# The second layer's input projection in another column order, with the indexer between its pieces and two conditioning items loaded elsewhere

## The chip, the cores and the metric

The kernel runs on one core of one Trainium2 chip. The metric is the device time of one execution in microseconds (us). Five engines take part: TensorE (PE in the rows; its weight loads PEld), VectorE (DVE), ScalarE (ACT), GpSimd (POOL, hardly used here) and SyncE (SP), which issues nearly all of the transfers. Each engine runs its own instructions strictly in the order in which they were written and waits for others at semaphores.

## The reference

A model trunk of two layers for 256 tokens of width 1024, in fp32, with batch 1. Every sub-layer is RMSNorm, shift and scale from a conditioning vector `c`, the mixer or feed-forward part, a gate from `c`, and the residual. Layer 0 has dilated attention and an S5 state-space part, then a dense SwiGLU (width 2816). Layer 1, whose first half the change touches, is this:

```
proj = u @ w_in                                   # 1024 x 1880
q_r, q_n, ckv, k_r, q_i, k_i, w_i = split(proj)   # 256, 768, 256, 16, 512, 64, 8 columns
q_r = rope(q_r, 16 heads)   ckv = rms_norm(ckv, g_kv)   k_r = rope(k_r)
q_i = rope(q_i, 8 heads)    k_i = rope(k_i)             w_i = w_i * 8 ** -0.5
logits = einsum('bqhd,bsd->bqhs', q_i, k_i) * 64 ** -0.5
score  = einsum('bqh,bqhs->bqs', w_i, relu(logits)), causal
idx    = top_k(score, 64)                         # keys that a query may see
k_n, v = ckv @ w_uk, ckv @ w_uv                   # (the reference does this in latent form)
attention of 16 heads over the chosen keys; then @ w_out
```

After it comes a top-2-of-8 mixture of experts (width 3584 each) and a final norm.

## The kernel before

Weights pass through `ring`, five slots of 16 KB per partition (`NS0`), and two more (`ring_more`) in the experts. `item()` gives each weight piece the next slot in turn; SP issues the loads in one list, and each load first waits until the piece that last lay in its slot has been used. Wide products are made in three passes: a weight chunk is split into a high part (`high`, ACT, L1548: `w_hi`) and the rest (`low`, DVE, L1882: `w_lo`), and PE multiplies x_hi by w_hi, x_hi by w_lo and x_lo by w_hi (`mm3`, L783 to L785). There are four chunk buffers (`NB`), so ACT can convert chunk c of a piece only when PE is done with chunk c of the piece before. Each piece is one `item`: 8 rows of 128 inputs in four chunks of two; for two token tiles that makes 48 matmuls of the piece's width.

The order of the work is written out by hand for each engine. In time:

- Dense feed-forward of layer 0: a loop over 512-wide blocks (`ff_block`); it uses ring slots 4, 0 and 2. Slots 1 and 3 hold the conditioning items 12 and 13 (`ada_item`: 1024 x 512 pieces of `w_ada`), which PE multiplies with `c` (`matvec`, L808) before the loop. Item 13's `matvec` stands between the first gate product and the first up product; ACT copies its result out (`part_out`, L1490) before it converts the first up piece.
- Behind the loop: `matvec` of items 14 and 15, the last down product, the residual (DVE L1966, L1968), the norm (`norm_stats`, `norm_scale`, `norm_split`) and the shift and scale made from items 12 to 15.
- Layer 1's projection in six pieces in the order of the columns (`o_cols`): 256 (q_r), 384 and 384 (q_n), 272 (ckv, k_r), 512 (q_i), 72 (k_i, w_i). DVE applies rope to q between them (L1923 to L1928), ACT copies the rest out of PSUM.
- Then DVE finishes ckv and k_i, PE transposes ckv (L789), DVE copies it out with g_kv (L2189), PE makes k_n (L1204) and v (L1213), ACT and DVE copy them out. Then the indexer: ten transposes, eight heads of logits (L1236), relu on ACT (L1736), weighted sum on DVE (L2210, L2212), eight rounds of top-k on DVE (`max`, L2219, `match_replace`, L2223), and the mask (L2225 to L2227). Beside the top-k, PE transposes q and k and ACT copies them (L1740), and PE makes the first two heads' scores (`scores_pair`, L858).
- Attention in eight pairs of heads. DVE adds the mask and takes the maximum (`mask_max`, L1940), ACT takes the exponentials (`exps`, L1561), and so on; one conditioning item is multiplied in each pair. Then the output projection (L1289), the router, and eight experts of 21 weight pieces.

An fp32 matmul that is not of the three-pass kind is recorded twice in the trace: eight matmuls show as x16.

## Time and profile before

| What | us |
|---|---|
| median of 3 runs (range) | 1662.81 (1662.75 to 1663.93) |
| the profiled execution | 1659.71 |
| span of its core | 1657.9 |
| PE busy in the span | 1551.6 (94%) |
| DVE busy | 1259.0 (76%) |
| ACT busy | 1043.8 (63%) |
| mean granted TensorE clock | 0.975 of full |

The span is the time from the first to the last record of the core; 1.8 us of the execution lie around it. The chain of work that ended last lies on PE for 78% of the span, on DVE for 6% and on ACT for 5%. The experts alone fill 635 to 1658 us. The stretch that the change touches lies between 222 and 574 us: the start of the dense loop, its end at 418, the norm to 431, the projection to 480, keys, values and indexer to 523, attention to 574.

### The profile page before, as it was taken

Reading aid. Unit: us, or ns where it says so; the run is one execution under the profiler, and the core shown is the slowest. Engines: PE = TensorE matmul, PEld = TensorE weight load, DVE = VectorE, ACT = ScalarE, POOL = GpSimd, SP = SyncE. Lnnn points to the kernel's source line nnn. Section 1 sums busy time; section 2 is a strip of 40 time slices with the busy share of each in tenths; the row PEclk is TensorE's granted clock in tenths of the full one; section 3 lists DMA queues with packets and bytes.
Section 4 is the critical chain, followed back from the end, with each engine's and each line's share of the span. In section 5 each row is a group of like instructions: output and inputs, shape, how many; then the busy total and the mean of one; then the engine's idle time right before and its main releaser. Section 6 shows DMA issues by size and latency. Waiting matters only on the chain.

```text
span 1657.9 us, 22266 instructions
## 1 busy us (share of the span) xinstructions
PE 1551.6 (94%) x7619; PEld 1202.9 (73%) x7620; DVE 1259.0 (76%) x1719; ACT 1043.8 (63%) x1374; POOL 62.8 (4%) x90
## 2 busy tenths in 40 slices
PE   4899989999897888999999999999999999999997
PEld 2545468887764456888888888888888888888885
DVE  6896345443646237989989989989989989989987
ACT  3105444443425626778778778778778778778775
POOL 5251000000000000000000000000000000000000
PEclk9999999999888988999999999999999999999999
DMA  9635855545654837999999999999999999999970
GB/s 319 232 102 195 313 203 200 177 156 177 228 181 150 307 116 265 365 332 358 365 328 364 362 331 366 350 334 362 354 335 363 351 338 362 351 337 364 353 260 27
DMA packets 203752, 469.68 MB, mean 283 GB/s; under 512 B 5108, under 2 KB 11558, under 8 KB 203574
## 3 DMA queue, kind: packets, MB, share of 16 engines
q1 hardware_dynamic: 202656, 466.80, 77.9%
q0 software_dynamic: 400, 1.09, 0.3%
q10 hardware_dynamic: 646, 1.16, 0.2%
q8 instruction: 28, 0.46, 0.1%
q14 instruction: 22, 0.18, 0.0%
HBM read 467.98 MB, written 1.05 MB: 283 GB/s over the span
## 4 chain that ended last, share of the span: by engine, by line
PE 78%; DVE 6%; ACT 5%; issue 2%; DMA 0%; DVEq 0%; ACTq 0%
PE ps L783 22%; PE ps L785 21%; PE ps L784 21%; PE ps L789 2%; PE ps L1330 2%; DVE w_lo L1882 2%; PE ps L1289 2%; PE ps L1056 1%; ACT work L1778 1%; PE ps L808 1%; ACT w_hi L1548 1%; ACT uT L1561 1%; PE ps L828 1%; PE ps L1204 0%; PE ps L1399 0%
## 5 line engine op out<-in xcount | busy, mean ns | idle before, releaser
L1882 DVE TENSOR_TENSOR w_lo<-ring,w_hi 128x1024 fp32r<-128x1024 f32 (+2 forms) x576 | 667.4, 1192 | 116.3 <-ACT w_hi L1548 102.5
L1548 ACT ACTIVATE w_hi<-ring 128x1024 fp32r<-128x1024 f32 (+2 forms) x576 | 594.9, 1038 | 210.3 <-PE ps L785 206.7
L783 PE MATMUL ps<-w_hi,e_hi 128*128 128x512 f32 x896 | 356.6, 398 | 9.7 <-DVE w_lo L1882 9.7
L785 PE MATMUL ps<-w_hi,e_lo 128*128 128x512 f32 x896 | 350.5, 391 | 0.0
L784 PE MATMUL ps<-w_lo,e_hi 128*128 128x512 f32 x896 | 349.6, 390 | 0.0
L1882 DVE TENSOR_TENSOR w_lo<-ring_more,w_hi 128x1024 fp32r<-128x1024 f32 x192 | 228.8, 1220 | 40.5 <-ACT w_hi L1548 38.1
L1548 ACT ACTIVATE w_hi<-ring_more 128x1024 fp32r<-128x1024 f32 x192 | 201.6, 1067 | 70.6 <-PE ps L785 70.6
L783 PEld LDWEIGHTS ps<-w_hi,e_hi 128*128 128x128 f32 x896 | 168.8, 188 | 46.3 <-DVE w_lo L1882 13.2
L785 PEld LDWEIGHTS ps<-w_hi,e_lo 128*128 128x128 f32 x896 | 168.6, 188 | 36.7
L784 PEld LDWEIGHTS ps<-w_lo,e_hi 128*128 128x128 f32 x896 | 169.0, 189 | 33.6
L783 PE MATMUL ps<-w_hi,eT_hi 128*128 128x512 f32 x448 | 176.6, 394 | 5.7 <-DVE w_lo L1882 5.7
L784 PE MATMUL ps<-w_lo,eT_hi 128*128 128x512 f32 x448 | 174.6, 390 | 0.0
L785 PE MATMUL ps<-w_hi,eT_lo 128*128 128x512 f32 x448 | 174.6, 390 | 0.0
L783 PE MATMUL ps<-w_hi,x_hi 128*128 128x512 f32 (+4 forms) x288 | 104.2, 362 | 11.0 <-DVE x_lo L1917 6.5
L783 PEld LDWEIGHTS ps<-w_hi,eT_hi 128*128 128x128 f32 x448 | 84.1, 188 | 28.5 <-DVE w_lo L1882 11.8
L784 PE MATMUL ps<-w_lo,x_hi 128*128 128x512 f32 (+4 forms) x288 | 103.5, 359 | 0.0
L785 PE MATMUL ps<-w_hi,x_lo 128*128 128x512 f32 (+4 forms) x288 | 103.3, 359 | 0.0
L785 PEld LDWEIGHTS ps<-w_hi,eT_lo 128*128 128x128 f32 x448 | 84.1, 188 | 17.9
L784 PEld LDWEIGHTS ps<-w_lo,eT_hi 128*128 128x128 f32 x448 | 84.2, 188 | 16.5
L783 PEld LDWEIGHTS ps<-w_hi,x_hi 128*128 128x128 f32 x288 | 55.5, 193 | 19.4 <-issue 10.5
L808 PE MATMUL ps<-ring,c_col 128*32 128x512 f32 x384 | 50.3, 644 | 14.6 <-DMA ring<-in_w_ada 12.9
L785 PEld LDWEIGHTS ps<-w_hi,x_lo 128*128 128x128 f32 x288 | 55.7, 193 | 7.1
...
## 6 DMA issues: line engine op xcount, KB each, us to landing
...
```

The costliest lines, as they stand in the source:

```text
L783: mm(o, xh, wh, start=start, stop=False)
L784: mm(o, xh, wl, start=False, stop=False)
L785: return mm(o, xl, wh, start=False, stop=stop)
L789: return nc.tensor.transpose(o, i, ident[0:n, 0:n])
L808: w = mm(ps[bank][j:j + 32, :], c_col[:, k:k + 1].broadcast_to([P, 32]), ap[:, k, :], start=k < 4, stop=False, tile_position=(0, j))
L828: mm(ps[bank][:, :], sel_col.broadcast_to([P, P]), part, start=True, stop=True).then_inc(mod_summed, 1)
L1056: w = mm(ps[2 * n + t][:, :], catT[:, k, t * P:(t + 1) * P], ap[:, k, :], start=k == 4, stop=k == 3)
L1289: w = mm(ps[4 + 2 * n + t][:, :], ctxT[:, k, t * P:(t + 1) * P], ap[:, k, :], start=k == 0, stop=k == KD - 1)
L1330: w = mm(o, hn[:, t, d], sel[:, t, :], start=t == 0, stop=t == NT - 1)
L1548: fn(w, src, ACT.Copy).then_inc(hi_ready, 1)
L1561: w = fn(x, x, ACT.Exp, scale=SC, bias=stat[:, 12 + 2 * q + t:13 + 2 * q + t], **({"accum_out": stat[:, 18 + 2 * q + t:19 + 2 * q + t]} if ...
L1882: V.tensor_tensor(w_lo[0:n, c, 0:f], src, w_hi[0:n, c, 0:f].bitcast(F32), ALU.subtract).then_inc(lo_ready, 1)
```

## The change

The projection's 1880 columns are loaded in five pieces instead of six, in this order: q_i (512), then ckv, k_r, k_i and w_i together (344), then q in three pieces (352, 336, 336). PE transposes k_i and q_i after the third piece. The logits are made in four pairs of heads between the chunks of the last two pieces; ACT's relu and DVE's weighted sum stand between their conversions of those pieces. The top-k stands on DVE behind the weighted sum with nothing else of keys and values ahead of it. The copies of v, of the transposed ckv and of the keys' rope part go from DVE to ACT. On DVE and ACT the first piece (q_i) is split ahead of the residual and its norm. qiT, kiT and ckvT lie in another region, since the logits now run while x_hi and x_lo are in use. Conditioning items 14 and 15 take slots 1 and 3 and are loaded at the start of the dense loop; their `matvec` stays where it was. Item 13's `matvec` and its copy come after the first up product. Slot numbers of everything behind shift with it.

```diff
--- before
+++ after
...
+        qiT = WX.take(4, S)
+        kiT = WX.take(S)
+        ckvT = WX.take(2, S)
 
         W2 = Region(work, WORK, NT * D + 2 * KD * S)
...
         static_before = list(stream)
+        stream.clear()
+        n_then = n_item[0]
+        for (sec, half), back in zip(HALVES[2:4], (3, 1)):
+            n_item[0] = n_then - back
+            ada_item(1, sec, half)
+        n_item[0] = n_then
+        static_mid = list(stream)
...
-        for sec, half in HALVES[2:4]:
-            ada_item(1, sec, half)
-        o_cols = [(0, 256), (256, 384), (640, 384), (1024, 272), (1296, 512), (1808, 72)]
-        o_in = [item(A["o_w_in"][0, :, a:a + n], KD, n, "split") for a, n in o_cols]
+        NQI, NCK, NQ0, NQ1 = IH * HD, LAT + ROPE + HD + IH, 256 + 2 * NOPE, 7 * NOPE
...
+        def o_item(n, *cols):
+            s = n_item[0] % NS0
+            n_item[0] += 1
+            pieces, at_ = [], 0
+            for a, m in cols:
+                pieces.append((block_ap(s, KD, n)[:, :, at_:at_ + m], o_w_in[:, :, a:a + m]))
+                at_ += m
+            return (n, push(s, pieces, "split"))
+        o_qi = o_item(NQI, (1296, NQI))
+        o_ck = o_item(NCK, (1024, LAT + ROPE), (1808, HD + IH))
+        o_q = [o_item(NQ0, (0, NQ0)), o_item(NQ1, (NQ0, NQ1)), o_item(NQ1, (NQ0 + NQ1, NQ1))]
...
+            for e in static_mid:
+                load(e)
...
                 rows(q, (0, 1), n, (2, 3))
+                if first:
+                    pe.wait_ge(part_ready, 14)
                 ff_down(q + NCI, u0, first)
...
             rows_of(ff_first["gate"][2], 1, FW, 1, 1)
-            matvec(13, 6)
             pe.wait_ge(part_ready, 13)
             rows(ff_first["up"][2], (2, 3), FW, range(NCI))
-            pe.wait_ge(part_ready, 14)
+            matvec(13, 6)
             ff_block(0, True)
             with pe.Fori(1, FB - 2) as i:
                 ff_block(i, False)
...
-            for j, banks in enumerate(((0, 1), (2, 3), (4, 5), (6, 7), (0, 1), (2, 3))):
-                if j == 4:
-                    pe.wait_ge(rope_done, 6)
-                if j == 5:
-                    pe.wait_ge(nope_done, 6)
-                if j == 0:
-                    for t in range(NT):
-                        rows_of(o_in[0][1][2], banks[t], o_cols[0][1], t, 2)
+            o_rows = lambda it, banks, chunks=range(NCI): rows(it[1][2], banks, it[0], chunks)
+            for t in range(NT):
+                rows_of(o_qi[1][2], t, NQI, t, 2)
+            pe.wait_ge(mod_ready, 3)
+            o_rows(o_ck, (2, 3))
+            o_rows(o_q[0], (4, 5))
+            pe.wait_ge(ki_ready, 2)
+            pe.wait_ge(ckr_copied, 2)
+            for t in range(NT):
+                w = tr(ps[2][:, t * P:(t + 1) * P], k_iw[:, t, 0:2 * HD])
+            w.then_inc(idxT_done, 1)
+            pe.wait_ge(qi_ready, 2)
+            for pr in range(4):
+                for t in range(NT):
+                    w = tr(ps[pr // 2][:, (pr % 2) * S + t * P:(pr % 2) * S + (t + 1) * P],
+                           q_i[:, t, 2 * pr:2 * pr + 2, :].rearrange("p h d -> p (h d)"))
+                if pr % 2:
+                    w.then_inc(idxT_done, 1)
+            def logits(pr):
+                if pr == 0:
+                    pe.wait_ge(idxT_ready, 3)
                 else:
-                    if j == 1:
-                        pe.wait_ge(mod_ready, 3)
-                    rows(o_in[j][1][2], banks, o_cols[j][1], range(NCI))
-            pe.wait_ge(nope_done, 8)
+                    pe.wait_ge(relu_ready, 2 * pr)
+                for t in range(NT):
+                    for i in range(2):
+                        r = slice(HD * i, HD * i + HD)
+                        w = mm(ps[2 + i][:, KOFF[t]:KOFF[t] + KEYS[t]], qiT[r, pr, t * P:(t + 1) * P], kiT[r, 0:KEYS[t]],
+                               start=True, stop=True)
+                        if t == NT - 1:
+                            w.then_inc(logit_done, 1)
+            o_rows(o_q[1], (6, 7), (0, 1))
+            logits(0)
+            o_rows(o_q[1], (6, 7), (2,))
+            logits(1)
+            o_rows(o_q[1], (6, 7), (3,))
+            logits(2)
+            o_rows(o_q[2], (0, 1), (0,))
+            logits(3)
+            o_rows(o_q[2], (0, 1), (1, 2, 3))
+            pe.wait_ge(q_copied, 2)
+            pe.wait_ge(q_roped, 2)
             for t in range(NT):
                 pe.wait_ge(ckv_ready, t + 1)
...
+            pe.wait_ge(q_copied, 6)
+            pe.wait_ge(relu_ready, IH)
             for i in range(4):
                 t, half = i // 2, i % 2
                 for k in range(2):
...
             pending[0] = True
 
             pe.wait_ge(kn_ready, 4)
-            for pr in range(4):
-                for t in range(NT):
-                    w = tr(ps[4 + pr // 2][:, (pr % 2) * S + t * P:(pr % 2) * S + (t + 1) * P],
...
-            pe.wait_ge(idxT_ready, 3)
-            pe.wait_ge(v_ready, 4)
...
-                if i >= 2:
-                    pe.wait_ge(relu_ready, i - 1)
-                for t in range(NT):
...
-            pe.wait_ge(rope_done, 12)
+            pe.wait_ge(kr_set, 2)
             for i, src in enumerate((q_tok, kcat)):
                 for pr in range(8):
                     if i and pr % 2 == 0:
...
                     for t in range(NT):
                         w = tr(ps[4 + pr // 2][:, (pr % 2) * S + t * P:(pr % 2) * S + (t + 1) * P],
                                src[:, t, 2 * pr:2 * pr + 2, :].rearrange("p h d -> p (h d)"))
+                        release(w)
                     if pr % 2:
                         w.then_inc(qkT_done, 1)
+            pe.wait_ge(v_ready, 4)
             pe.wait_ge(qkT_ready, 12)
-            pe.wait_ge(relu_ready, IH)
             scores_pair(A_HEADS, qT1, kT1, 0, True)
 
...
                 if t:
                     part_out(12, parts1[:, 0, :], 2)
                 norm_hi(1, t)
-            part_out(13, parts1[:, 1, :], 6)
             item_high(ff_first["up"][2], *ff_first["up"][:2], ff_chunk_of(FW))
             act.wait_ge(chunk_done, NCI)
             silus(0)
+            part_out(13, parts1[:, 1, :], 6)
...
+            o_high(o_qi)
             norm_stats(2)
-            proj_end = lambda j: o_in[j][1][2] + NCI
...
+            for t in range(NT):
+                norm_hi(2, t)
+            o_high(o_ck)
+            o_rows_done(o_qi)
+            for t in range(NT):
+                fn(q_i[:, t, :, ROPE:], heads(ps[t][:, :], 8)[:, :, ROPE:], ACT.Copy).then_inc(qi_copied, 1)
+            o_high(o_q[0])
+            o_rows_done(o_ck)
+            for t in range(NT):
+                fn(ckr[:, t, :], ps[2 + t][:, 0:LAT + ROPE], ACT.Copy).then_inc(ckr_copied, 1)
...
+            o_high(o_q[1], (0, 1))
+            q_out(0, (4, 5), 256, 0, 2)
+            o_high(o_q[1], (2,))
+            for i in range(2):
+                act.wait_ge(idxT_done, i + 2)
+                fn(qiT[:, 2 * i:2 * i + 2, :], ps[i][:, :].rearrange("p (c s) -> p c s", c=2), ACT.Copy).then_inc(idxT_ready, 1)
+            o_high(o_q[1], (3,))
+            o_high(o_q[2], (0,))
+            relu(0)
+            relu(1)
+            o_high(o_q[2], (1, 2))
+            relu(2)
+            relu(3)
+            o_high(o_q[2], (3,))
+            relu(4)
+            relu(5)
+            q_out(1, (6, 7), 0, 2, 7)
+            relu(6)
+            relu(7)
+            for k in range(2):
+                act.wait_ge(ckvT_done, 1)
+                fn(ckvT[:, k, :], ps[4][:, k * S:(k + 1) * S], ACT.Copy, scale=g_kv[:, k:k + 1]).then_inc(ckvT_ready, 1)
+            q_out(2, (0, 1), 0, 9, 7)
+            for t in range(NT):
+                act.wait_ge(kr_ready, t + 1)
+                fn(kcat[:, t, :, 0:ROPE], kr_t[:, t, :].unsqueeze(1).broadcast_to([P, C_HEADS, ROPE]), ACT.Copy).then_inc(kr_set, 1)
...
+            for i in range(4):
+                t, half = i // 2, i % 2
+                act.wait_ge(kv_done, 5 + i)
+                fn(v1[:, t, half * 512:(half + 1) * 512], ps[i][:, :], ACT.Copy).then_inc(v_ready, 1)
             for i in range(8):
                 act.wait_ge(qkT_done, 5 + i)
                 dst = (qT1, kT1)[i // 4]
                 fn(dst[:, 2 * (i % 4):2 * (i % 4) + 2, :], ps[4 + i % 4][:, :].rearrange("p (c s) -> p c s", c=2),
                    ACT.Copy).then_inc(qkT_ready, 1)
+            fn(stat[:, 30:31], eps[:, 0:1], ACT.Exp)
             exps(A_HEADS, True)
...
-            for t in range(NT):
-                residual(t, 4, 1, (4 + 2 * t, 5 + 2 * t))
-            for t in range(NT):
-                dve.wait_ge(h_ready, 4 + 2 * t + 2)
-                norm_scale(2, t, 5 + t)
-            columns(0, 1, 10, 2)
...
+            o_low(o_qi)
+            for t in range(NT):
+                residual(t, 4, 1, (4 + 2 * t, 5 + 2 * t))
+            for t in range(NT):
+                dve.wait_ge(h_ready, 4 + 2 * t + 2)
+                norm_scale(2, t, 5 + t)
+            columns(0, 1, 10, 2)
+            dve.wait_ge(mod_ready, 3)
+            for t in range(NT):
+                norm_split(2, t)
+            o_low(o_ck)
+            q_index(0)
+            o_low(o_q[0], (0,))
+            q_index(1)
+            o_low(o_q[0], (1, 2, 3))
+            dve.wait_ge(ckr_copied, 2)
+            for t in range(NT):
+                k_index(t)
+            o_low(o_q[1], (0, 1))
+            for t in range(NT):
+                k_rope(t)
+                ckv_norm(t)
+            o_low(o_q[1], (2,))
+            dve.wait_ge(idxT_done, 1)
+            V.tensor_copy(kiT[:, :], ps[2][:, 0:S]).then_inc(idxT_ready, 1)
+            o_low(o_q[1], (3,))
+            q_rope(0)
+            o_low(o_q[2], (0,))
+            q_rope(1)
+            add_score(0)
+            add_score(1)
+            o_low(o_q[2], (1, 2))
+            add_score(2)
+            add_score(3)
+            o_low(o_q[2], (3,))
+            for i in range(4, IH):
+                add_score(i)
```

SP's list of loads, around the start and the end of the dense loop, before:

```order
L620 DMA ring<-in_ff_w_gate 128x8x512 [waits lo_ready]
L620 DMA ring<-in_ff_w_down 128x4x1024 [waits weights_used]
L620 DMA ring<-in_ff_w_up 128x8x512 [waits lo_ready]
...
L599 DMA ring<-in_ff_w_down 128x2x1024 [waits lo_ready]
L599 DMA ring<-in_w_ada 128x8x512 [waits lo_ready] x2
L599 DMA ring<-in_o_w_in 128x8x256 [waits ada_done]
```

and after:

```order
L644 DMA ring<-in_ff_w_gate 128x8x512 [waits lo_ready]
L644 DMA ring<-in_ff_w_down 128x4x1024 [waits weights_used]
L644 DMA ring<-in_ff_w_up 128x8x512 [waits lo_ready]
L623 DMA ring<-in_w_ada 128x8x512 [waits ada_done] x2
...
L623 DMA ring<-in_ff_w_down 128x2x1024 [waits lo_ready]
L623 DMA ring<-in_o_w_in 128x8x512 [waits lo_ready]
```

The two `w_ada` loads (items 14 and 15) stood at the end behind the last down piece and waited for the slots of gate and up; now they stand ahead of the loop, and the projection's first piece follows the down piece.

DVE between the last down product and the transposed norm, before:

```order
L1882 TENSOR_TENSOR w_lo<-ring,w_hi 128x512 [waits hi_ready] x4
L1966 TENSOR_TENSOR ps<-ps,gate_row 128x512 [waits gate_ready,chunk_done]
L1968 TENSOR_TENSOR h<-h,ps 128x512 [waits dve_steps]
...
L1874 COPY mod_b<-ps 128x8 [waits mod_summed]
L1875 SCALAR_TENSOR_TENSOR mod_a<-ps,g_col 128x8
L1882 TENSOR_TENSOR w_lo<-ring,w_hi 128x512 [waits hi_ready,mod_ready]
L1882 TENSOR_TENSOR w_lo<-ring,w_hi 128x512 [waits hi_ready] x3
L1908 TENSOR_SCALAR uT<-ps,mod_a,mod_b 128x128 [waits hnT_done]
```

and after:

```order
L1949 TENSOR_TENSOR w_lo<-ring,w_hi 128x512 [waits hi_ready] x4
L1949 TENSOR_TENSOR w_lo<-ring,w_hi 128x1024 [waits hi_ready,chunk_done]
L1949 TENSOR_TENSOR w_lo<-ring,w_hi 128x1024 [waits hi_ready] x3
L2033 TENSOR_TENSOR ps<-ps,gate_row 128x512 [waits gate_ready]
L2035 TENSOR_TENSOR h<-h,ps 128x512 [waits dve_steps]
...
L1941 COPY mod_b<-ps 128x8 [waits mod_summed]
L1942 SCALAR_TENSOR_TENSOR mod_a<-ps,g_col 128x8
L1975 TENSOR_SCALAR uT<-ps,mod_a,mod_b 128x128 [waits hnT_done,mod_ready]
```

The split of the projection's first piece has moved from behind the scale (`mod_a`) to ahead of the residual (`h`), and is 1024 instead of 512 elements wide per chunk.

PE between the projection and the attention's first scores, before (L1204 makes k_n, L1213 v, L1236 logits, L789 transposes, L858 scores):

```order
L1204 MATMUL ps<-ring,work 128x384 [waits slot2_filled,nope_done,ckvT_ready]
L1204 MATMUL ps<-ring,work 128x384 x7
L1213 MATMUL ps<-ring,work 128x512 [waits nope_done,rope_done]
L1213 MATMUL ps<-ring,work 128x512 x7
L789 MATMUL ps<-cst,work 128x128 [waits kn_ready]
L789 MATMUL ps<-cst,work 128x128 x9
L1236 MATMUL ps<-work 128x128 [waits v_ready,idxT_ready]
...
L789 MATMUL ps<-cst,work 128x128 [waits rope_done]
L789 MATMUL ps<-cst,work 128x128 x15
...
L858 MATMUL ps<-ada 128x128 [waits relu_ready,qkT_ready]
```

and PE in the projection after the change (L810 is a three-pass matmul, L816 a transpose, L1235 a logit; numbers are those of PSUM banks and buffers):

```order
L816 MATMUL ps2<-cst,work_52 128x128 [waits ckr_copied,ki_ready]
...
L816 MATMUL ps0<-cst,work_52 128x128 [waits qi_ready]
...
L810 MATMUL ps6<-w_hi_54,x_hi_56 128x336 [waits lo_ready]
...
L1235 MATMUL ps2<-ada_50 128x128 [waits idxT_ready]
L1235 MATMUL ps3<-ada_50 128x128
L1235 MATMUL ps2<-ada_50 128x256
L1235 MATMUL ps3<-ada_50 128x256
L810 MATMUL ps6<-w_hi_54,x_hi_56 128x336 [waits lo_ready]
...
L1235 MATMUL ps2<-ada_50 128x128 [waits relu_ready]
```

The transposes and the logits stood behind v and waited for its copies; now they stand among the projection's chunks and wait for the indexer's own work and for relu.

## Rows read from the trace of the kernel before

**Rows 1.** Windows: busy us of each engine, granted clock, DMA share, GB/s.

```profile
431.30:480.10 48.80, 47.24 (x289) 44.81 (x290) 24.97 (x55) 20.39 (x40) 0.00 (x0) 0.96 0.57 192
480.10:522.60 42.50, 29.14 (x143) 17.23 (x142) 27.90 (x113) 12.14 (x23) 0.00 (x0) 0.82 0.39 138
522.60:574.00 51.40, 45.33 (x408) 24.67 (x408) 15.05 (x93) 40.32 (x132) 0.00 (x0) 0.92 0.78 279
635.50:1657.90 1022.40, 1000.18 (x4616) 824.14 (x4616) 921.24 (x941) 797.28 (x887) 0.00 (x0) 0.99 0.91 331
```

**Rows 2.** Timeline of PE, first matmul of the first up product.

```profile
234.79 0.47 PE L783 MATMUL ps<-w_hi,x_hi 128*128 128x512 f32 x1 [3.01 <-DVE w_lo L1882]
```

**Rows 3.** Timeline of PE at the dense loop's end: item 15.

```profile
407.34 1.06 PE L808 MATMUL ps<-ring,c_col 128*32 128x512 f32 x8 [1.52 <-DMA ring<-in_w_ada]
```

**Rows 4.** Timeline of DVE: splits of 1024-wide and 512-wide chunks; the residual's start.

```profile
385.50 4.63 DVE L1882 TENSOR_TENSOR w_lo<-ring,w_hi 128x1024 fp32r<-128x1024 f32 x4
...
417.85 0.70 DVE L1966 TENSOR_TENSOR ps<-ps,gate_row 128x512 f32<-128x512 f32 x1 [4.10 <-PE ps L785]
...
426.01 2.49 DVE L1882 TENSOR_TENSOR w_lo<-ring,w_hi 128x512 fp32r<-128x512 f32 x4
```

**Rows 5.** Timeline of PE: first matmuls of five of the projection's pieces.

```profile
431.32 0.39 PE L783 MATMUL ps<-w_hi,x_hi 128*128 128x256 f32 x1 [3.46 <-DVE x_lo L1917]
...
448.05 0.33 PE L783 MATMUL ps<-w_hi,x_hi 128*128 128x384 f32 x1
...
456.37 0.28 PE L783 MATMUL ps<-w_hi,x_hi 128*128 128x272 f32 x1
...
462.35 0.39 PE L783 MATMUL ps<-w_hi,x_hi 128*128 128x512 f32 x1
...
473.28 0.20 PE L783 MATMUL ps<-w_hi,x_hi 128*128 128x72 f32 x1
```

**Rows 6.** Short windows for the granted clock.

```profile
431.30:434.70 3.40, 3.38 (x16) 3.40 (x17) 2.70 (x7) 2.21 (x6) 0.00 (x0) 0.53 0.74 216
...
473.30:479.20 5.90, 4.98 (x45) 4.87 (x44) 3.70 (x18) 2.68 (x10) 0.00 (x0) 1.00 0.24 50
479.20:483.70 4.50, 1.93 (x10) 1.53 (x9) 3.17 (x22) 0.00 (x0) 0.00 (x0) 0.51 1.04 388
483.70:488.00 4.30, 4.25 (x7) 2.41 (x8) 2.13 (x14) 0.49 (x1) 0.00 (x0) 0.50 0.15 54
```

**Rows 7.** The chain of waits: k_n, v, one group of logits.

```profile
483.75 8.27 PE ps L1204 x16
492.03 6.87 PE ps L1213 x16
...
500.51 0.93 PE ps L1236 x8
```

**Rows 8.** Groups of PE by line and form, 489 to 512 us: transposes.

```profile
L789 PE MATMUL ps<-cst,work 128*128 128x128 f32 x42 | 5.0, 274 | 0.0
```

**Rows 9.** Timeline of ACT: copies of the transposed q and k.

```profile
507.26 4.03 ACT L1740 ACTIVATE ada<-ps 128x512 f32<-128x512 f32 x8
```

**Rows 10.** Timeline of DVE: weighted sum, top-k, mask, first maximum.

```profile
503.55 4.66 DVE L2212 SCALAR_TENSOR_TENSOR work<-uT,work 128x128 f32<-128x128 f32 x12 [0.24 <-ACT uT L1736]
508.25 0.56 DVE L2215 TENSOR_TENSOR work<-work,cst 128x384 f32<-128x384 f32 x1
...
520.35 0.36 DVE L2225 TENSOR_SCALAR work<-work 128x384 f32<-128x384 f32 x1
...
521.73 0.29 DVE L1940 CUSTOM_DVE_ANT_0 uT<-ps,work 128x128 f32<-128x128 f32 x1
```

**Rows 11.** The chain of waits: exponentials of the first pair and of two later ones.

```profile
522.61 1.86 ACT uT L1561 x8
...
535.88 1.74 ACT uT L1561 x8
...
541.84 1.75 ACT uT L1561 x8
```

157 lines of the change are left out of this document (51 added, 106 removed).

## The prediction

> **What bounds the kernel now.** I read the windows first, stretch by stretch, and then the chain of waits inside each. The experts, 635 to 1658 us, are bound by PE: 1000 of 1022 us busy [rows 1]. Nothing in the change touches their work, so what they take now they take afterwards. From 431 to 480 us, the projection, PE is busy 47.2 of 48.8 us: again PE. From 480 to 523 us it isn't: PE is busy 29.1 of 42.5 us, DVE 27.9, ACT 12.1 [rows 1], since each waits for another in turn. The chain there has k_n (8.3 us), v (6.9 us), then logits and their weighted sum [rows 7, 10], and then DVE alone: the top-k and the mask from 508.25 to 521.73, 13.5 us in which PE runs out of work [rows 10]. The attention begins when ACT starts its first exponentials at 522.61 [rows 11]. So I ask when that moment comes after the change; all that follows depends on it, up to the output. I use the profiled execution's clock throughout.
>
> **Item 13 behind the first up product.** Before, PE makes item 13's product with `c` first and then waits 3.01 us for the up piece's first split [rows 2], because ACT copies item 13 out before it converts. After, the up product starts at once. But then come item 13's matmuls, its copy on ACT, and only behind that copy ACT converts the next gate piece and DVE splits it: the same chain of copy, conversion and split, so the same 3.0 us, one product later. ACT's first conversion of the loop is what is queued behind its new wait, and PE waits for it. Sum: **0**.
>
> **Items 14 and 15 loaded early.** Their loads now run at the start of the dense loop, where PE sets the pace. At the loop's end PE stands still for 1.52 us until item 15 has landed [rows 3]. With the loads gone from there, **-1.5**, and the last down product ends at 416.3 instead of 417.8 [rows 4]. What is late next there is ACT's conversion of the down piece behind the two copies, a wait that stays as it is. The projection's loads stand higher in SP's list than before, so they are no bound.
>
> **The first split ahead of the residual.** DVE now splits q_i's four chunks before it starts the residual, 4.6 us for 1024-wide ones instead of 2.5 us for 512-wide ones further down [rows 4]. Both lie on the chain: **+2.1**. The projection starts at 431.3 - 1.5 + 2.1 = 431.9.
>
> **The projection.** From the start of one piece to the next, 384 columns take 8.32 us, 272 take 5.98 and 512 take 10.93 [rows 5]: 0.0204 us for each column of a piece. The last piece is off that line: by it 72 columns would take 1.9 us, and they take 6.8, to 480.1, so a narrow piece is dear. After: 10.93 for q_i, and 7.50, 7.67, 7.34 and 7.34 for widths 344, 352, 336 and 336, together 40.8. The first 3.4 us go at the lower clock level as before [rows 6], 1.7 us lost, and I add 1.2 for waits and restarts (PE's idleness was 1.6 in this stretch [rows 1]): 43.7 us for 48.8 before, **-5.1**. Into it go ten transposes at 0.12 us [rows 8] and four groups of logits at 0.93 [rows 7]: **+4.9**. The projection ends at 480.5, within 0.4 us of before, and now holds the logits.
>
> Whether PE waits in it is decided on ACT and DVE. They were busy 20.4 and 25.0 of 48.8 us [rows 1], and get eight relus at some 0.5 us, the price of a 512-wide copy [rows 9], and eight weighted sums at 0.78 (twelve instructions, two to a head, in 4.66 us) [rows 10], besides work on k_i and ckv. That leaves a quarter of DVE's time free. I followed the queues, chunk by chunk: the relu of heads 4 and 5 waits for DVE's sums, which stand behind q's rope and two splits, and PE's last logits wait about 0.3 us. That is inside the 1.2.
>
> **From the projection's end to the first exponentials.** Before, 42.5 us, from 480.1 to 522.6. After, on PE and ACT: ckv's four transposes 0.5 [rows 8], ACT's two copies with g_kv and the handovers 1.1 (estimated from [rows 9]), k_n 5.2, v 6.9 [rows 7], the copy of v's last part 0.6, eight copies of q and k in a row on ACT 4.0 [rows 9], scores 0.9 like a group of logits, maximum 0.9 (from 521.73 to 522.61). Sum 20.1, that is **-22.4**. For k_n I take 16 records at 0.323 us, v's 0.429 [rows 7] times 384/512; before, it took 8.3 us, as the granted clock was 0.5 over its first half [rows 6]. DVE needs 12.1 us for the top-k and 1.4 for the mask [rows 10]; the weighted sum ends near 477, so the mask is ready near 490.5, and the scores come near 499.5. The top-k is covered with 9 us to spare. What is last now is PE's k_n and v, then ACT's copies.
>
> **The first pairs of heads.** A pair's exponentials follow those of the pair before by 5.96 us, but the first two pairs take 13.2 us together [rows 11]; PE had stood still during the top-k and came back slow. After, PE is busy up to there: **-1.3**.
>
> **Sum.** 0 - 1.5 + 2.1 - 5.1 + 4.9 - 22.4 - 1.3 = -23.3 us. The span goes from 1657.9 to 1634.6 and the profiled execution from 1659.7 to 1636.4. The median of the runs shown is 3.1 us above the profiled one; taken from it, the forecast is **1639.5**.
>
> **A rule against it.** The rows show PE at full clock with 0.9 us of idleness in 5.9, and right behind it at half, until into k_n [rows 6]; what it did before the fall was the 72-column piece. The Trainium skill, page "TensorE: Matmul & The Clock Gate", section "A second HAM failure mode: psum-queue depth-cycling", says that short idle times between groups of matmuls can make the clock swing between its levels, and the change puts such waits into the projection. By the row's full clock the sum is as above; by that rule it is the first or the third rival below. The trace agrees in so far as the fall came after short waits.
>
> **Rivals.**
> - *The clock stays low over k_n, v and the first pair.* k_n and v took 15.1 us before [rows 7] against 12.1 at full clock, and the pairs lose their 1.3: +4.3, 1643.8. For it: the trace shows this at this very place. Against it: the narrow piece and PE's long wait for DVE ahead of k_n are gone.
> - *PE waits at the logits.* Each group after the first needs two relus, each behind a weighted sum, and DVE has splits and rope ahead of those. If DVE runs two 672-wide splits (0.76 each, by width from [rows 4]) later than I have it, all three groups wait 1.5 us: +4.6, 1644.1. Against it: a quarter of DVE free. That the top-k isn't hidden after all would need DVE to be 9 us late; I count that here too.
> - *Slower: the lower level holds through the projection.* The waits at transposes and logits make the clock fall near 445 us, and each of PE's 36 us from there to 480 and the 12 of k_n and v takes twice as long: +48, 1687. It is slower than before from the point where 23.3 us of PE's work in the stretch run at half. Against it: the waits inside the projection (1.6 us in all) left the mean clock there at 0.96 [rows 1].
> - *DMA paces the gain away.* In the attention each pair needs one load of 2.1 MB; at this stretch's 279 GB/s [rows 1] that is 7.5 us, against 5.96 for a pair. If the last four pairs wait for theirs: +6, 1645.5. Against it: the loads are issued five pairs ahead, and slots come free earlier too.
>
> **How the numbers follow.** Forecast 0.60, low clock at k_n and v 0.15, waits at the logits 0.14, DMA 0.06, slower 0.03, and 0.02 that these eat each other up to no change. The forecast's own bounds: 3 us down, if handovers are shorter and no idleness stays, and 3 up. To hold 8 in 10 the range reaches to the first two rivals and to their parts together: **1635.5 to 1647**. A measurement of this kernel tells 0.2%, some 3.3 us, from no change. Faster 0.95, same 0.02, slower 0.03.
>
> **What would show it.** In the profile after: no DMA in the chain at the dense loop's end; the first exponentials near 500.5; no wait of PE above 1 us between 432 and 480; the last `match_replace` some 9 us ahead of the first scores; k_n in 5.2 us at granted clock 1.0; pairs 5.9 us apart from the first on; the experts' stretch as long as before. Wrong would be: a granted clock of 0.5 anywhere between 436 and 530, PE waiting more than 1 us for a relu, or the first exponentials later than 505.

## The result, and the profile after

The changed kernel takes 1637.5 us, the median of four executions (1632.4 to 1639.1), against 1663.4 for the kernel before on the same chip (1662.8 to 1666.0): a ratio of 0.984, 95% interval 0.982 to 0.986. The forecast was 1639.5. The profiled execution took 1632.35 us with a span of 1630.5, 27.4 less than before; it is the fastest of the four, so its stages add up to more than the 25.8 us between the medians. Two executions lie outside all comparisons here and below, since their granted clock was low from end to end (2616.8 us at 0.56, 2002.6 us at 0.74). The table sets the stages beside those of before; a stage ends where the next begins.

| Stage | before | after | difference | forecast |
|---|---|---|---|---|
| start to the S5 part (unchanged code) | 61.5 | 58.7 | -2.8 | 0 |
| S5 part to the dense loop | 160.9 | 160.9 | 0 | 0 |
| dense loop, with item 13, to item 14 | 181.3 | 181.3 | 0 | 0 |
| items 14 and 15, to the last down product | 8.4 | 6.7 | -1.7 | -1.5 |
| last down product | 5.7 | 7.3 | +1.6 | 0 |
| its end to the projection's first matmul | 13.5 | 15.9 | +2.4 | +2.1 |
| projection, with transposes and logits after | 48.9 | 46.4 | -2.5 | -0.2 |
| its end to the first exponentials | 42.4 | 20.3 | -22.1 | -22.4 |
| eight pairs of heads | 51.5 | 50.0 | -1.5 | -1.3 |
| output projection, router, experts | 1083.8 | 1083.1 | -0.7 | 0 |

Windows of the changed kernel (busy us of PE, PEld, DVE, ACT, POOL; granted clock, DMA share, GB/s): the projection, from there to the first exponentials, the attention, the experts. They answer to [rows 1].

```profile
430.70:477.20 46.50, 46.45 (x284) 42.38 (x285) 35.85 (x112) 22.71 (x46) 0.00 (x0) 1.00 0.52 180
477.20:497.40 20.20, 18.07 (x88) 10.69 (x90) 10.22 (x45) 11.89 (x24) 0.00 (x0) 1.00 0.28 95
497.40:547.40 50.00, 43.62 (x428) 23.80 (x419) 14.92 (x94) 40.20 (x133) 0.00 (x0) 1.00 0.95 334
608.90:1630.50 1021.60, 999.59 (x4616) 823.93 (x4616) 921.48 (x941) 797.39 (x887) 0.00 (x0) 0.99 0.91 332
```

PE is busy for 46.45 of 46.50 us of the projection: it waits nowhere in it, though DVE has gone from 25.0 to 35.9 us of work there [rows 1]. Behind it PE is busy 89% of the time where it was 69%.

The chain of waits, from the projection's end on (start us, us, what): ckv's transposed copies, k_n, v, eight copies of q and k, the scores, and exponentials of three pairs. It answers to [rows 7, 11].

```profile
477.67 0.85 ACT ada L1790 x2
...
478.56 5.43 PE ps L1264 x16
483.99 6.88 PE ps L1273 x16
...
491.49 3.93 ACT ada L1806 x8
...
495.55 0.95 PE ps L885 x8
...
497.46 1.86 ACT uT L1601 x8
...
503.38 1.74 ACT uT L1601 x8
...
509.24 1.74 ACT uT L1601 x8
```

There is no top-k in it. DVE's timeline tells where it went: splits of q_i, the causal term ahead of the top-k, the last step of the mask, and the first maximum. It answers to [rows 4, 10].

```profile
414.90 4.63 DVE L1949 TENSOR_TENSOR w_lo<-ring,w_hi 128x1024 fp32r<-128x1024 f32 x4 [5.70 <-PE ps L812]
...
473.67 0.56 DVE L2298 TENSOR_TENSOR work<-work,cst 128x384 f32<-128x384 f32 x1
...
486.76 0.36 DVE L2310 TENSOR_SCALAR work<-work 128x384 f32<-128x384 f32 x1
...
496.57 0.29 DVE L2007 CUSTOM_DVE_ANT_0 uT<-ps,work 128x128 f32<-128x128 f32 x1 [9.46 <-PE ps L885]
```

The top-k begins at 474.3, while PE is still in the projection; the mask is ready at 487.1, and DVE then stands idle for 9.46 us until PE has the scores. PE's timeline at the three places where the conditioning items and the first split act (answers to [rows 2, 3, 5]):

```profile
242.84 0.47 PE L810 MATMUL ps<-w_hi,x_hi 128*128 128x512 f32 x1 [3.01 <-DVE w_lo L1949]
...
402.82 1.90 PE L835 MATMUL ps<-ring,c_col 128*32 128x512 f32 x16
...
407.55 0.47 PE L810 MATMUL ps<-w_hi,mT_hi 128*128 128x512 f32 x1 [2.02 <-DVE w_lo L1949]
...
430.75 0.47 PE L810 MATMUL ps<-w_hi,x_hi 128*128 128x512 f32 x1 [1.52 <-DVE x_lo L1984]
```

The 3.0 us wait is there again, one product later. Item 15 no longer waits for a DMA. The two waits behind it are for DVE's splits, of a weight chunk (`w_lo`) and of the normed input (`x_lo`).

### The profile page after: what moved, and what is told of

It reads as the page before. It is cut to its first block, busy times and chain, and to the rows that moved or that the text cites. A ratio compares the mean times of both kernels' runs of the same rounds, so it can differ in the third digit from the quotient of the medians.

```text
span 1630.5 us, 22147 instructions
## 1 busy us (share of the span) xinstructions
PE 1538.7 (94%) x7571; PEld 1195.2 (73%) x7572; DVE 1254.6 (77%) x1707; ACT 1048.2 (64%) x1381; POOL 62.8 (4%) x90
## 4 chain that ended last, share of the span: by engine, by line
PE 81%; ACT 5%; DVE 4%; issue 2%; ACTq 0%; DVEq 0%
PE ps L810 23%; PE ps L812 22%; PE ps L811 22%; PE ps L816 2%; PE ps L1370 2%; DVE w_lo L1949 2%; PE ps L1329 2%; PE ps L1083 1%; ACT work L1845 1%; PE ps L835 1%; ACT uT L1601 1%; ACT w_hi L1588 1%; ACT uT L1610 1%; PE ps L1439 0%; PE ps L1440 0%
## 5 line engine op out<-in xcount | busy, mean ns | idle before, releaser
L810 PE MATMUL ps<-w_hi,e_hi 128*128 128x512 f32 x896 | 356.6, 398 | 9.7 <-DVE w_lo L1949 9.7
L810 PEld LDWEIGHTS ps<-w_hi,e_hi 128*128 128x128 f32 x896 | 168.9, 189 | 46.3 <-DVE w_lo L1949 13.2
L810 PE MATMUL ps<-w_hi,eT_hi 128*128 128x512 f32 x448 | 176.5, 394 | 5.7 <-DVE w_lo L1949 5.7
L810 PE MATMUL ps<-w_hi,x_hi 128*128 128x512 f32 (+4 forms) x272 | 99.8, 367 | 7.6 <-DVE x_lo L1984 4.5
L810 PEld LDWEIGHTS ps<-w_hi,eT_hi 128*128 128x128 f32 x448 | 84.1, 188 | 28.3 <-DVE w_lo L1949 11.9
L812 PE MATMUL ps<-w_hi,x_lo 128*128 128x512 f32 (+4 forms) x272 | 98.7, 363 | 0.0
L811 PE MATMUL ps<-w_lo,x_hi 128*128 128x512 f32 (+4 forms) x272 | 98.5, 362 | 0.0
L810 PEld LDWEIGHTS ps<-w_hi,x_hi 128*128 128x128 f32 x272 | 51.6, 190 | 16.6 <-issue 9.7
L835 PE MATMUL ps<-ring,c_col 128*32 128x512 f32 x384 | 48.9, 629 | 13.6 <-DMA ring<-in_w_ada 11.8
L811 PEld LDWEIGHTS ps<-w_lo,x_hi 128*128 128x128 f32 x272 | 51.7, 190 | 6.9
```

The source lines that it names most:

```text
L810: mm(o, xh, wh, start=start, stop=False)
L811: mm(o, xh, wl, start=False, stop=False)
L812: return mm(o, xl, wh, start=False, stop=stop)
L835: w = mm(ps[bank][j:j + 32, :], c_col[:, k:k + 1].broadcast_to([P, 32]), ap[:, k, :], start=k < 4, stop=False, tile_position=(0, j))
```

## The experiments

**A second trace of the changed kernel**, to see which stages repeat.

> The changed kernel once more, unchanged, for a second trace. In the first pair of traces 2.8 us of the 27.4 lie ahead of all changed code (the S5 part begins at 58.7 us instead of 61.5), and the clock fell once at the down product of the loop's end (408.4 to 411.8 us, some 1.6 us lost). Theory A, chance: the falls of the granted clock come at other moments in each execution, so here the S5 part begins anywhere between 58 and 62 us and the down product takes 5.7 or 7.3 us, while the stretches without a fall (the dense loop 181.3 us, first exponentials to output projection 50.0) repeat within 0.3 us; the time lies between 1632 and 1640. Theory B, tied to the code: both stand at the same places again, 58.7 and 7.3 us, and the projection again shows full clock from its first matmul.

Measured: 1637.2 us (1636.5 to 1637.4), 0.985 of before (0.983 to 0.987). The S5 part begins at 60.2 us. The down product takes 7.3 again, down product's end to projection 15.9, the projection 46.4, its end to the exponentials 20.3, the pairs 49.9. So everything from the down product's end to the attention's end repeats to 0.05 us, and the start of S5 does not: in the traces of this study, whose code is the same up to there, it lies between 58.7 and 61.5. The product ahead of it begins between 46.8 and 47.4 us in every trace, and after that the granted clock stays at 0.50 for 5.6 us in the trace before, 3.4 in this one and not at all in the first trace of the changed kernel. So the 2.8 us of the first row of the table are chance, and they are the clock's; the kernel before fell at the high end and the changed one at the low. Against the expectation the dense loop does not repeat either: it took 182.6 us for 181.3, with 6.1 us at 0.50 at its start for 3.4. What follows the attention took 1083.9 for 1083.1. On the down product neither theory is settled yet.

**The conditioning items alone**, in the kernel before (`static_mid` holds the loads of items 14 and 15 and stands ahead of the dense loop on SP; item 13's copy on ACT moves as in the change):

```diff
+            for e in static_mid:
+                load(e)
...
-            matvec(13, 6)
             pe.wait_ge(part_ready, 13)
             rows(ff_first["up"][2], (2, 3), FW, range(NCI))
-            pe.wait_ge(part_ready, 14)
+            matvec(13, 6)
```

> The kernel before with only the conditioning items changed as in the change: 14 and 15 loaded at the start of the dense loop, item 13's product and copy behind the first up product. Theory (the prediction's terms): item 13 is worth 0, since PE's 3.0 us wait for the first split comes back one product later (dense loop from its first gate product to item 14's product: 181.3 us as before); items 14 and 15 are worth -1.5, since the 1.52 us DMA wait ahead of item 15 is gone (item 14's product to the last down product 6.7 to 6.9 us instead of 8.4). All behind it unchanged: about -1.5 us, 1661.9. Rival, clock: PE's shorter pause there lets the clock fall in the last down product, which then takes 7.3 instead of 5.7 us: 0 in all, 1663.4. Rival, DMA: the two loads take the loop's own loads time, and the loop becomes longer by up to two loads' time, 10 us: 1672.

Measured: 1661.5 us against 1661.6, ratio 0.999 (0.998 to 1.000): no gain that can be measured. In the trace the wait for the DMA is gone, as in the changed kernel, but the clock fell in the down product that follows. PE's timeline and a window of it:

```profile
407.27 1.90 PE L816 MATMUL ps<-ring,c_col 128*32 128x512 f32 x16
...
411.99 0.47 PE L791 MATMUL ps<-w_hi,mT_hi 128*128 128x512 f32 x1 [2.02 <-DVE w_lo L1891]
```

```profile
412.00:416.80 4.80, 4.80 (x14) 3.83 (x15) 1.65 (x3) 2.16 (x4) 0.00 (x0) 0.65 0.72 225
```

Item 14's product to the last down product took 6.7 us for 8.4 (-1.7), the down product 7.3 for 5.7 (+1.6). That is the clock rival's 0. The rival of the loads is out: the loop took 182.8 us here, within the 181.3 to 185.2 of the traces with and without them. The two edits give 1.7 us of waiting back, and in this trace the clock takes it. The trace as a whole is 2.5 us longer than the one before, by stages that the edits don't touch: the projection took 51.4 us for 48.9, as the granted clock rose later in its first piece and fell earlier in its last. Whether the gain must be lost stays open: with the DMA wait in place the down product ran at full clock in two traces of three, without it in two of nine.

**The narrow piece alone.** The kernel before, with k_i and w_i beside ckv and k_r:

```diff
-        o_cols = [(0, 256), (256, 384), (640, 384), (1024, 272), (1296, 512), (1808, 72)]
+        o_cols = [(0, 256), (256, 384), (640, 384), (1024, 344), (1296, 512)]
...
+        o_in = [o_item(n, (a, n)) if n != 344 else o_item(n, (1024, 272), (1808, 72)) for a, n in o_cols]
```

> The kernel before with one thing of the change alone: the 72 columns of k_i and w_i ride with ckv and k_r (344 columns), so that the projection has five pieces instead of six, in the old order; indexer, keys, values and top-k stay where they are. The rope and the copy of q_i, which stood beside the narrow piece, come after the projection, beside ckv's transposes and k_n. Theory (the prediction's term): the projection shrinks by 5.1 us, from 48.9 to 43.8, and what was hidden beside the narrow piece stays hidden beside k_n (5 to 8 us of PE): -5.1, 1658.3. Theory, clock: the narrow piece was what preceded the fall of the clock over ckv's transposes and k_n; without it k_n takes 5.4 instead of 8.3 us: -8, 1655.4. Rival: q_i's copies and rope (1.7 + 3 us) now delay k_n or v: -1, 1662.

DVE's work on k_i now stands further ahead, and the rope and copy of q_i come behind the projection. Measured: 1653.5 us (1652.2 to 1654.4), ratio 0.995 (0.993 to 0.996), -8.1 us. The projection took 43.5 for 48.9 us, -5.4, and from its end to the exponentials it was 37.4 for 42.4, -5.0. The chain of waits behind it, and a window:

```profile
480.03 0.45 PE ps L801 x4
...
480.50 0.89 DVE work L2201 x2
...
481.44 5.43 PE ps L1215 x16
486.86 6.87 PE ps L1224 x16
```

```profile
480.00:487.00 7.00, 6.03 (x22) 3.57 (x21) 5.34 (x28) 2.45 (x6) 0.00 (x0) 1.00 0.06 19
```

k_n takes 5.43 us where it took 8.27 [rows 7], at a granted clock of 1.00 where it was 0.51 [rows 6]: that is 2.8 of the 5.0 us. The other 2.1 lie between the projection's end and k_n, 1.41 us for 3.54. Before, k_i came last, so DVE made its rope and its copies there, ahead of copying the transposed ckv; PE's narrow piece and that copy of DVE, in the kernel before:

```profile
476.96 0.30 PE L783 MATMUL ps<-w_hi,x_hi 128*128 128x72 f32 x1 [0.92 <-DVE w_lo L1882]
```

```profile
482.72 0.19 DVE L2186 COPY work<-work 128x64 f32<-128x64 f32 x1
482.83 0.87 DVE L2189 TENSOR_SCALAR work<-ps,g_kv 128x256 f32<-128x256 f32 x2
```

The first of these lines shows that the narrow piece's 6.8 us are not all width: at full clock its matmuls follow at 0.11 us, 5.3 for the 48, PE waits 0.92 us in it for a split that stands behind q's rope on DVE, and the rest is the lower clock at its end. All three kernels here that keep the 72-column piece have that wait of 0.92 us and show the clock falling while PE was in that piece (at 479.3, 478.3 and 480.9 us; the piece ended at 480.2, 484.3 and 481.3); of the nine traces without it, only the next experiment's shows a fall around k_n. Whether the narrow matmuls or the wait among them bring the fall no run separates; the merge removes both. So a third of the change's gain needs no new order at all: it is one piece less.

**The logits behind the projection.** The changed kernel with its four groups of logits, relus and sums out of the chunks (PE's part of the edit):

```diff
-            o_rows(o_q[1], (6, 7), (0, 1))
-            logits(0)
...
-            o_rows(o_q[2], (0, 1), (1, 2, 3))
+            o_rows(o_q[1], (6, 7))
+            pe.wait_ge(idxT_ready, 3)
+            o_rows(o_q[2], (0, 1))
+            for pr in range(4):
+                logits(pr)
```

> The changed kernel with the four groups of logits, their relus and weighted sums behind the projection instead of among its chunks; the transposes of k_i and q_i stay inside it, the order of columns stays. Theory: among the chunks the logits cost PE just their own 3.7 us and no waits; behind it they run at the pace of relu and weighted sum, some 2 us for a pair of heads. The projection ends 3.7 us earlier, the four groups take 7 us on PE, and all behind them moves back by 3.3 us: first exponentials 300.8 us after the S5 part's end of PE work moves to 3.3 us later than in the changed kernel, 1640.8. The top-k then ends some 1 to 3 us ahead of the scores, still covered. Rival, the top-k is the bound again: weighted sums at the pace of DVE end so late that top-k and mask end behind the scores; first exponentials 6 us later, 1643.5. Rival, interleaving itself costs PE (restarts, lower clock): no difference or a gain, 1636 to 1637.5.

Measured: 1643.1 us (1642.3 to 1644.5) for 1637.2, +6.0. By the number alone this is the rival in which the top-k bounds. The trace says otherwise. PE's timeline: four groups of logits, k_n, the scores:

```profile
476.58 0.93 PE L1235 MATMUL ps<-ada 64*128 64x128 f32 x8
...
478.46 0.93 PE L1235 MATMUL ps<-ada 64*128 64x128 f32 x8 [0.95 <-ACT uT L1741]
...
480.34 1.40 PE L1235 MATMUL ps<-ada 64*128 64x128 f32 x8 [0.95 <-ACT uT L1741]
...
482.69 1.65 PE L1235 MATMUL ps<-ada 64*128 64x128 f32 x8 [0.95 <-ACT uT L1741]
...
486.32 7.68 PE L1260 MATMUL ps<-ring,ada 128*128 128x384 f32 x16 [0.93 <-ACT ada L1778]
...
505.56 0.93 PE L885 MATMUL ps<-ada 64*128 64x128 f32 x8 [1.20 <-ACT ada L1794]
```

```profile
480.60:490.90 10.30, 8.42 (x27) 4.60 (x26) 8.05 (x28) 4.37 (x11) 0.00 (x0) 0.50 0.00 1
```

DVE's last step of the mask and its first maximum:

```profile
499.61 0.36 DVE L2293 TENSOR_SCALAR work<-work 128x384 f32<-128x384 f32 x1
506.58 0.29 DVE L1995 CUSTOM_DVE_ANT_0 uT<-ps,work 128x128 f32<-128x128 f32 x1 [6.62 <-PE ps L885]
```

The mask was ready at 499.97 and DVE then stood idle for 6.62 us, so the top-k was covered here too. The four groups took 7.7 us (I had 7), three waits of 0.95 us among them. And the granted clock fell to the lower level at 480.6, behind the first two of these waits, and stayed there into k_n, which took 7.68 us instead of 5.43. From the projection's start to the first exponentials it took 72.9 us for the 66.7 of the changed kernel. Among the chunks the groups cost 4.3 us (the projection takes 46.4 with them and 42.1 without), behind it 7.7, and the copy of ckv and k_n behind them took 0.6 and 2.2 longer: 7.7 - 4.3 + 0.6 + 2.2 = 6.2. Of the 7.7, 2.9 are the three waits and about 1.2 the lower clock in the last two groups. So the expected cause, the pace of relu, explains about half, and the other half is the clock, which the expectation had left out. What the interleaving buys is the relu waits, and a clock that stays up. The Trainium skill, page "TensorE: Matmul & The Clock Gate", section "A second HAM failure mode: psum-queue depth-cycling", says that short idle times between groups can make the clock swing; this trace agrees, with 0.50 behind waits of 0.95 us. The changed kernel, where the waits are absent, doesn't show it.

**How much the top-k is covered.** Extra pairs of `max` ahead of its rounds, 0.66 us each, their results overwritten: 9 pairs (5.9 us) and 24 (15.9 us) in the changed kernel, 9 in the kernel before. Each was executed once, and the readings are of stages in its trace.

```diff
+            for _ in range(9):
+                for t in range(NT):
+                    step(V.max(top8[:, t, :], score[:, KOFF[t]:KOFF[t] + KEYS[t]]))
+                step.wait()
             for i in range(TOPK // 8):
```

> The changed kernel with nine extra pairs of the top-k's maximum ahead of its eight rounds (their results are overwritten): 0.66 us each, 5.9 us more on DVE. In the changed kernel's trace the mask was ready at 487.1 us and the first scores at 496.5, 9.4 us of slack. Theory, the top-k is covered: no change, last score of the projection's end to the first exponentials 20.3 us, the time 1637. Rival, the slack is apparent, and the first exponentials depend on DVE's end by something else: up to +5.9, 1643.

> The same with 24 extra pairs, 15.9 us more on DVE. Theory: 9.4 us of it is covered and 6.5 are not: projection's end to first exponentials 26.8 instead of 20.3 us; PE, out of work for so long, comes back at the lower clock, which costs the first pairs up to 1.5 us more; the time 1643.5 to 1645. Rival, the cover is smaller because PE's scores or ACT's copies need DVE earlier: +10 or more, 1647.

> The kernel before with the nine extra pairs of the top-k's maximum, 5.9 us more on DVE. Theory: there the top-k is the chain, so every microsecond shows: projection's end to the first exponentials 42.4 + 5.9 = 48.3 us, about 1668; in the changed kernel the same addition showed 0. Over ckv's transposes and k_n the clock is at half again, as in both traces of kernels with the narrow piece (479 to 489 us), and k_n takes 8.3 us. Rival: the clock's low stretch there was chance, k_n takes 5.4 us, and the stretch is 45.5 us.

| Kernel | projection's end to first exponentials | added | shown |
|---|---|---|---|
| changed | 20.26 | 0 | 0 |
| changed, 9 pairs | 20.26 | 5.9 | 0.0 |
| changed, 24 pairs | 26.57 | 15.9 | 6.3 |
| before | 42.39 | 0 | 0 |
| before, 9 pairs | 46.87 | 5.9 | 4.5 |

The whole times were 1638.7, 1644.6 and 1665.0 us, the last beside a median of 1664.3 for the kernel before on the same chip, whose executions spread from 1657.2 to 1669.2: one time of a kernel can't show 4.5 us there, the stage can.

DVE's timeline, 9 and then 24 pairs in the changed kernel: the last step of the mask and the first maximum.

```profile
497.22 0.36 DVE L2314 TENSOR_SCALAR work<-work 128x384 f32<-128x384 f32 x1
501.14 0.29 DVE L2007 CUSTOM_DVE_ANT_0 uT<-ps,work 128x128 f32<-128x128 f32 x1 [3.56 <-PE ps L885]
```

```profile
506.43 0.36 DVE L2314 TENSOR_SCALAR work<-work 128x384 f32<-128x384 f32 x1
506.82 0.29 DVE L2007 CUSTOM_DVE_ANT_0 uT<-ps,work 128x128 f32<-128x128 f32 x1
```

The slack shrinks from 9.46 to 3.56 us, by the 5.9 added, and nothing moves. With 15.9 it is used up, and the rest shows: 15.9 - 9.46 = 6.4, measured 6.3. The pairs then took 51.3 us for 50.0, at a clock of 0.50 from 505.1 to 515.3, so that 1.3 us of the gain at the first pairs hangs on PE not running dry ahead of them. In the kernel before the same 5.9 us come out as 4.5, where 5.9 were expected, since k_n took 6.84 us instead of 8.27 in that trace:

```profile
484.82 6.84 PE L1204 MATMUL ps<-ring,work 128*128 128x384 f32 x16 [2.63 <-DVE work L2189]
```

5.9 - 1.43 = 4.47: without the clock's share the delay shows in full.

**Place or width of the first split.** The changed kernel with q_i's splits behind the norm's scale:

```diff
-            o_low(o_qi)
             for t in range(NT):
                 residual(t, 4, 1, (4 + 2 * t, 5 + 2 * t))
...
             columns(0, 1, 10, 2)
             dve.wait_ge(mod_ready, 3)
+            o_low(o_qi)
```

> The changed kernel with the four splits of q_i's chunks on DVE back behind the residual, the norm's scale and mod_a, where the first piece's splits stood before; all else as in the change. In three traces of kernels with the change's order the stretch from the last down product's end to the projection's first matmul took 15.9 us, in the kernel before 13.5. Theory, width: DVE is the chain through the whole stretch, so it is the four splits' length (4.6 us at 1024 wide for 2.5 at 512) that costs 2.1 to 2.4 us and not their place; the stretch stays at 15.6 to 15.9 us and the time at 1637.2. Theory, place: the splits delay the residual and with it the norm's work on ACT and PE; put behind, they lie partly beside that work, and the stretch shrinks to 13.5, the time to 1634.8.

Measured: 15.64 us for 15.89 from the down product's end to the projection; 1638.2 us (1637.0 to 1639.2), ratio 0.985 (0.983 to 0.988) to before, as the changed kernel has. It is the width: 15.64 is 2.13 more than the 13.51 of before, and the splits differ by 4.63 - 2.49 = 2.14 [rows 4]; their place makes 0.25. DVE has work nearly all the way, with waits of 0.75 and 0.69 us, and four 1024-wide splits cost 4.63 us wherever they stand:

```profile
426.19 4.63 DVE L1949 TENSOR_TENSOR w_lo<-ring,w_hi 128x1024 fp32r<-128x1024 f32 x4
430.73 1.36 DVE L1975 TENSOR_SCALAR uT<-ps,mod_a,mod_b 128x128 f32<-128x128 f32 x4
```

**The first split beside the down product.** DVE waits for the whole down product only ahead of the residual:

```diff
-            dve.wait_ge(chunk_done, ff_last["down"][2] + NCI)
...
             o_low(o_qi)
+            dve.wait_ge(chunk_done, ff_last["down"][2] + NCI)
             for t in range(NT):
                 residual(t, 4, 1, (4 + 2 * t, 5 + 2 * t))
```

> The changed kernel with one wait of DVE moved: it splits q_i's four chunks as soon as ACT has converted each, beside the last down product (ACT's conversions in the changed kernel's trace: 409.8, 412.2, 413.5, 414.9 us, the down product ends at 414.9), and waits for the whole down product only ahead of the residual. Theory: three of four splits are covered by the down product in which DVE stood idle for 5.7 us, and one, 1.2 us, stays: end of the down product to the projection's start 15.9 - 3.5 = 12.4 us, the time 1633.7. Rival, the chain has a second leg as long (ACT's norm statistics, PE's columns): only some 2 us, 14 us, 1635.2. Rival, clock: PE then pauses for less, and the clock's fall moves into the projection's start, 1.7 us lost there: 1635.4.

> The kernel with the splits of q_i beside the last down product once more, for a trace: the one recorded before was taken while the clock was at 0.56 over the whole execution (2615 us) and says nothing of the stages; its other executions gave 1637.0. Theory: down product's end to the projection's start 12.4 us instead of 15.9, and the time 3.5 us below the changed kernel's on the same chip. Rival, second leg: 14 us. Rival, clock: the stretch is shorter, but the clock falls into the projection's start or the down product more often and takes 2 us back.

The stages are read from the second run's trace. Measured in the second: 1636.1 us (1634.6 to 1637.6), ratio 0.983 (0.980 to 0.986), and 1637.0 in the first, ratio 0.984 (0.982 to 0.987). The stretch is 13.6 us, not 12.4. DVE's timeline:

```profile
414.44 1.23 DVE L1949 TENSOR_TENSOR w_lo<-ring,w_hi 128x1024 fp32r<-128x1024 f32 x1 [1.52 <-ACT w_hi L1588]
416.88 1.23 DVE L1949 TENSOR_TENSOR w_lo<-ring,w_hi 128x1024 fp32r<-128x1024 f32 x1 [1.22 <-ACT w_hi L1588]
418.35 2.58 DVE L1949 TENSOR_TENSOR w_lo<-ring,w_hi 128x1024 fp32r<-128x1024 f32 x2 [0.24 <-ACT w_hi L1588]
420.85 0.69 DVE L2033 TENSOR_TENSOR ps<-ps,gate_row 128x512 f32<-128x512 f32 x1
```

The down product ended at 418.58. Two splits are covered, the last two are not, since ACT can convert the fourth chunk only when PE has left its buffer: 2.3 us gained instead of 3.5. And the projection was at 0.50 from 432.2 to 436.3 and took 48.4 us for 46.4, so that in this trace nearly all of the gain is lost in the next stage, as the clock rival had it. That the earlier start is the reason is not shown: with 9 extra pairs and with the split behind the scale, where the projection starts no earlier than 15.6 us behind the down product, it too began at 0.50, for 4.3 and 5.5 us. The ratios, 0.983 and 0.984 against the changed kernel's 0.984 and 0.985, can't tell this kernel from it.

**Three moves on top of the change.** This first split; ACT's first dense block written out, with item 13's copy (`part_out(13, ...)`, asked for by `first`) behind its gate conversions; at the loop's end ACT's conversion of the down piece ahead of the copies, and PE's transposes between items 14 and 15:

```diff
             matvec(14, 0)
+            ff_T((FB - 1) * NT, FL)
             matvec(15, 1)
-            ff_T((FB - 1) * NT, FL)
...
-            part_out(13, parts1[:, 1, :], 6)
-            with act.Fori(0, FB - 2) as i:
+            ff_block(0, first=True)
+            with act.Fori(1, FB - 2) as i:
...
+            item_high(ff_last["down"][2], *ff_last["down"][:2], ff_half_chunk)
             part_out(14, parts1[:, 2, :], 0)
+            midT_high((FB - 1) * NT, FL)
             part_out(15, parts1[:, 3, :], 1)
-            midT_high((FB - 1) * NT, FL)
-            item_high(ff_last["down"][2], *ff_last["down"][:2], ff_half_chunk)
```

> The changed kernel with three moves. One: DVE splits q_i's chunks beside the last down product. Two: ACT's first block of the dense loop stands alone, with the copy of item 13 behind the conversions of its gate piece, so that PE's 3.0 us wait for the first split behind item 13's product goes. Three: at the loop's end ACT converts the last down piece ahead of the copies of items 14 and 15, and PE transposes between the two products, so that its 2.0 us wait goes. Theory: -3.5, -3.0 and -2.0, 8.5 us in all; first gate product to item 14's product 179.5 instead of 182.5 us, item 14's product to the last down product 4.6 instead of 6.7, the down product's end to the projection 12.4 instead of 15.9; the time 1628.7. Rival, DMA: the loop's loads pace it once PE no longer waits, and move two gives nothing: 1631.7. Rival, clock: the falls move into busier places and take back 2 us: 1630.7.

Measured: 1629.4 us (1625.2 to 1630.8), ratio 0.979 (0.976 to 0.982) to before: the fastest of all. It is 34.9 us under the kernel before on the same chip, where the changed kernel was 25.8 and 24.5 under, so the three moves bring some 9 to 10 us; an estimate, since no chip ran both. Dense loop to item 14: 179.4 us for the 181.3 to 182.9 of the changed order; item 14 to the down product 4.7 for 6.7; down product's end to the projection 13.6 for 15.9. PE's timeline has no wait left at the loop's end:

```profile
404.41 1.92 PE L835 MATMUL ps<-ring,c_col 128*32 128x512 f32 x16
...
406.48 0.50 PE L810 MATMUL ps<-w_hi,mT_hi 128*128 128x512 f32 x1
```

The projection took 48.3 us again, with 3.9 us at the lower level. Of the rivals the loads are out: they don't pace the loop. The clock took back 1.8 us in the projection, but the down product ran at full clock in this trace, 5.7 us for 7.3, which gives 1.6 back.

## Why the prediction was right, point by point

- **What bounds.** PE before 480 and behind 635, the serial top-k between: confirmed by the same addition of 5.9 us, which shows before (4.5 us, and in full when k_n's shorter time in that trace is taken off) and not at all after.
- **Item 13: 0.** Right, with the 3.01 us wait at the place named: the pause around the product is 5.09 us long in both kernels. The loop as a whole varies from 181.3 to 185.2 us between traces, so that its equal length in the first two is luck. That it could be had for -3 with another order on ACT was not seen.
- **Items 14 and 15: -1.5.** The wait's size was right (-1.7), its worth was not: the down product behind it went from 5.7 to 7.3 us at a lower clock in seven traces of nine, and the edits alone measured 0. The step counted the wait and not what the clock does behind it.
- **First split: +2.1.** 2.4, and by the width, as the working had it.
- **Projection: -5.1 and +4.9.** The merge by itself gave -5.4. Together they gave -2.5 instead of -0.2. Two terms were put too high: 1.2 us of waits, of which there were none, and 1.7 us for the lower clock at the start. One was too low: the groups of logits cost 4.3 us among the chunks and not 3.7. In the changed kernel's two traces, and in two of the six traces of its variants (24 pairs, logits behind), the clock was up before the first matmul (at 428.9 for 430.75, 432.5 for 434.0). In the other four it rose 3.9 to 5.5 us into the projection, which then took 48.3 to 49.0, the forecast's 48.6. So the lower clock costs about 2 us in half of the traces, 1 us in the mean, and this trace was on the lucky side. The prediction also took the 6.8 us of the 72-column piece for the price of its width; 0.9 of them are a wait for DVE, and part is the lower clock.
- **Projection's end to the exponentials: -22.4.** -22.1, and item by item: k_n 5.43 (5.2), v 6.88 (6.9), copies 3.93 (4.0), scores 0.95 (0.9). The mask had 9.46 us to spare (9). But one part of this term isn't the top-k's: the merge alone, with the top-k still in the chain, brought 5.0 of it, 2.8 because k_n ran at full clock and 2.1 because DVE's work on k_i no longer stood ahead of ckv's copy. The prediction had the first in its 5.2 us for k_n and the second in its 1.6 us for ckv's transposes and copies, and didn't say that both come with the merge.
- **First pairs: -1.3.** -1.5; the pairs follow at 5.9 us from the first on.
- **The sum** was -23.3. From the dense loop's first matmul on, the two traces differ by 24.5, the terms above and -0.7 in what follows; the other 2.9 lie ahead of it, in unchanged code. That it comes so near is partly luck: the terms of items 14 and 15 (forecast -1.5, with the down product -0.1) and of the projection (forecast -0.2, measured -2.5) are off in opposite ways. The medians differ by 25.8 and, in the second comparison, 24.5.
- **Rivals.** The clock did not stay low over k_n in any trace of the changed kernel, and the first exponentials came at 497.5 and 500.7 us. PE did not wait at the logits. The lower level through the projection did not come. DMA was at 0.95 of its time in the attention (334 GB/s for 279) without one wait of PE for it. The conditions named for the first and third are real, though: with waits put in (logits behind the projection) the clock fell right behind the second.

By the parts, then: conditioning items 0, the piece less -8, and about -17 for the new order, of which 6 hang on the logits standing between the chunks. The -17 is what is left of the whole; no run has the new order with six pieces.
